# A gated-linear-attention stage with its recurrence in groups of four chunks, and its first projections by halves of the tokens

## The reference

```
def gla_mixer(h, w_in, w_gate2, b_gate, norm_w, w_out):
    proj = h @ w_in
    q, k, v, r, glr = jnp.split(proj, ...)          # glr has rank 16
    log_a = jax.nn.log_sigmoid(glr @ w_gate2 + b_gate) / GLA_TAU
    g = jnp.cumsum(lac, axis=2)                     # within a chunk
    k_dec = kc * jnp.exp(g_end[:, :, None] - g)
    def body(state, inp):                           # over the 16 chunks
        state = state * jnp.exp(ge_c)[..., None] + jnp.einsum('bshk,bshv->bhkv', kd_c, v_c)
        o = jnp.einsum('bqhk,bhkv->bqhv', q_c, state)
        return state, o
    o = rms_normalize(from_chunks(o)).reshape(b_, l_, hv) * norm_w
    return (o * jax.nn.silu(r)) @ w_out
```

## Time and profile before

| | us |
|---|---|
| median of three runs | 2855.92 (2855.51 to 2856.86) |
| profiled execution | 2854.91 |
| its span | 2853.1 |
| TensorE busy in the span | 2756.6 (97%) |
| TensorE busy in 0 to 60 us | 46.50 |
| TensorE busy in 440 to 450 us, granted clock | 5.08, 0.90 |
| TensorE busy in 450 to 460 us, granted clock | 7.48, 0.50 |

### The profile page before, as it was taken

One profiled execution on the slowest core, in us unless ns is written; L12 is line 12 of the kernel. 1 busy time (PEld: TensorE's weight loads), 2 busy tenths in 40 slices (PEclk: granted clock), 3 DMA queues, 4 the chain that ended last, 5 costly groups with the idle time before them and its releaser, 6 DMA issues. The chain is left out here.

```text
span 2853.1 us, 38388 instructions
## 1 busy us (share of the span) xinstructions
PE 2756.6 (97%) x13551; PEld 2276.0 (80%) x13551; DVE 1553.9 (54%) x1958; ACT 1047.5 (37%) x1526; POOL 1611.6 (56%) x1096
## 2 busy tenths in 40 slices
PE   8999998999999999899999999999998999999998
PEld 6888886788888888678778778778786888888887
DVE  5334335455555645667667666667634544444445
ACT  4313315432333323644444444544524322222223
POOL 3333334777677776866466565565435655565552
PEclk9999998999999999999999999999999999999999
DMA  3111110112112121212111121121430211122112
GB/s 122 38 45 37 37 44 0 52 45 66 44 51 59 44 66 44 94 47 64 41 53 57 38 63 49 45 63 49 155 111 16 59 59 37 51 59 59 37 51 96
DMA packets 200726, 160.23 MB, mean 56 GB/s; under 512 B 6231, under 2 KB 176812, under 8 KB 200621
## 3 DMA queue, kind: packets, MB, share of 16 engines
q1 hardware_dynamic: 200621, 158.83, 18.5%
HBM read 143.08 MB, written 15.73 MB: 56 GB/s over the span
## 5 line engine op out<-in xcount | busy, mean ns | idle before, releaser
L339 POOL TENSOR_TENSOR w_lo<-w_raw,w_hi 128x512 fp32r<-128x512 f32 x272 | 384.6, 1420 | 238.2 <-ACT w_hi L333 238.2
L443 PE MATMUL PA<-h_hi,w_hi 128*128 128x512 f32 x816 | 331.6, 406 | 17.7 <-PEq L929 5.9
L445 PE MATMUL PA<-h_hi,w_lo 128*128 128x512 f32 x816 | 321.0, 393 | 0.0
L444 PE MATMUL PA<-h_lo,w_hi 128*128 128x512 f32 x816 | 320.5, 393 | 0.0
L339 POOL TENSOR_TENSOR w_lo<-f_sums,w_hi 128x512 fp32r<-128x512 f32 x114 | 186.4, 1635 | 172.7 <-ACT w_hi L333 172.7
L333 ACT CAST w_hi<-w_raw 128x512 fp32r<-128x512 f32 x272 | 164.0, 617 | 228.1 <-DMA w_raw<-in_w_in 118.6
L443 PE MATMUL PB<-f_t_hi,w_hi 128*128 128x512 f32 x544 | 215.5, 396 | 9.3 <-ACT hy_tm L2523 5.0
L445 PE MATMUL PB<-f_t_hi,w_lo 128*128 128x512 f32 x544 | 212.6, 391 | 0.0
L444 PE MATMUL PB<-f_t_lo,w_hi 128*128 128x512 f32 x544 | 212.3, 390 | 0.0
L339 POOL TENSOR_TENSOR w_lo<-w_lo_raw,w_hi 128x512 fp32r<-128x512 f32 x108 | 139.8, 1300 | 115.7 <-ACT w_hi L333 115.7
L443 PEld LDWEIGHTS PA<-h_hi,w_hi 128*128 128x128 f32 x816 | 155.1, 190 | 54.5 <-issue 13.8
(11 more groups left out here) (543 smaller groups left out, 7177.7 us busy)
## 6 DMA issues: line engine op xcount, KB each, us to landing
w_raw<-in_w_in SPq DMA_DIRECT2D x64, 512.0 KB, 5.3
w_raw<-in_ffn_w_up SPq DMA_DIRECT2D x42, 512.0 KB, 5.0
w_lo_raw<-in_w_down SPq DMA_DIRECT2D x64, 256.0 KB, 2.6
w_raw<-in_w_up SPq DMA_DIRECT2D x30, 512.0 KB, 5.3
w_raw<-in_gla_w_in SPq DMA_DIRECT2D x24, 512.0 KB, 3.8
w_lo_raw<-in_ffn_w_down SPq DMA_DIRECT2D x44, 256.0 KB, 2.6
X<-in_x SPq DMA_DIRECT2D x8, 512.0 KB, 7.4
w_raw<-in_gla_w_out SPq DMA_DIRECT2D x8, 512.0 KB, 3.5
```

Source lines behind the costliest of these rows:

```text
L339: pool.tensor_tensor(lo, source, hi.bitcast(F32), ALU.subtract).then_inc(self.split, 1)
L443: pe.matmul(bank, ah[:, k, :], bh[:, k, :], start=(k == 0 and not more), stop=False, skip_group_check=more)
L444: pe.matmul(bank, ah[:, k, :], bl[:, k, :], start=False, stop=False, skip_group_check=more)
L445: mm = pe.matmul(bank, al[:, k, :], bh[:, k, :], start=False, stop=(k == 3), skip_group_check=more)
```

## The change

The steps of the recurrence become groups of four chunks. `ORDER` has `C0` to `C4` in place of `C0` to `C8`: four updates in `C0`, four reads and four updates in `C1` to `C3`, four reads in `C4`. They stand two `r` tiles apart. The states of a group have four slots, which lie in `T3`; `DD` and `MM` hold four results each; ScalarE squares two tiles and takes two roots in one operation.

In the first stage the low-rank product of the first 512 tokens is laid between the transposes of the last tiles, in two parts, into `PB`. The key product of head 0's first half comes right behind the last transposes, ahead of the second half of the low-rank product, and the first gate comes after the first two of eight parts of the second half of the keys.

```diff
-            ORDER = ("k.0 C8* YR* gate k.1 YT0* v.0 v.1 YT1* v.2 v.3 dn* q.0 q.1 KT r.0 C0 r.1 C1 r.2 C2 r.3 C3 "
-                     "r.4 C4 r.5 C5 r.6 C6 YRa r.7 C7").split()
+            ORDER = ("k.0 C4* YR* gate k.1 YT0* v.0 v.1 YT1* v.2 v.3 dn* q.0 q.1 KT r.0 C0 r.1 r.2 C1 r.3 r.4 C2 "
+                     "r.5 YRa r.6 C3 r.7").split()
+            GROUP = 4
+            GROUPS = NCH // GROUP
+            def state_bank(n):
+                return c.DD[:, n % 2 * HALF + n % GROUP // 2 * DV:n % 2 * HALF + n % GROUP // 2 * DV + DV]
+            def out_bank(m):
+                return c.MM[:, m % GROUP * DV:(m % GROUP + 1) * DV]
...
-                head.tensor(pe, lambda m: None)
+                for m in range(MT - 2):
+                    norm.turn(pe, m)
+                pe.wait_ge(norm.lo, MT // 2)
+                pe.wait_ge(s["g_lo"], 1)
+                rank(0, range(KT // 2))
+                norm.turn(pe, MT - 2)
+                rank(0, range(KT // 2, KT))
+                norm.turn(pe, MT - 1)
+                key(0, range(KT))
                 pe.wait_ge(s["rows_in"], 16 * 14)
+                pe.wait_ge(norm.lo, MT - 1)
...
                 pe.wait_ge(norm.lo, MT)
-                pe.wait_ge(s["g_lo"], 1)
-                for half in range(2):
-                    cols = slice(half * HALF, (half + 1) * HALF)
-                    for k in range(KT):
-                        mm = product(pe, c.MM[:, cols], (ghi[:, k, :], glo[:, k, :]),
-                                     (c.hhi[:, k, cols], c.hlo[:, k, cols]), k == 0, k == KT - 1)
-                mm.then_inc(s["glr_mm"], 1)
+                rank(1, range(KT)).then_inc(s["glr_mm"], 1)
+                key(1, range(2))
                 pe.wait_ge(s["glr"], 1)
                 pe.wait_ge(s["params"], 1)
+                gate(0)
+                key(1, range(2, KT)).then_inc(st.used, 1)
...
                 def update(h, n):
-                    if n >= 2:
+                    if n >= GROUP and n % GROUP < 2:
                         pe.wait_ge(s["s"], h * NCH + n - 1)
...
                 def read(h, n):
                     pe.wait_ge(s["s"], h * NCH + n + 1)
                     m = n // 2
-                    if m >= 2:
-                        pe.wait_ge(s["o_n"], h * MT + m - 1)
+                    if m >= GROUP:
+                        pe.wait_ge(s["o_n"], h * MT + m // 2 * 2 - 2)
...
-                            read(h, 2 * m - 2)
-                            read(h, 2 * m - 1)
-                        if m < MT:
-                            update(h, 2 * m)
-                            update(h, 2 * m + 1)
+                            for n in range(GROUP * (g - 1), GROUP * g):
+                                read(h, n)
+                        if g < GROUPS:
+                            for n in range(GROUP * g, GROUP * (g + 1)):
+                                update(h, n)
...
+                def squares(h, g):
+                    act.wait_ge(s["o_mm"], h * NCH + GROUP * (g + 1))
+                    for m in (2 * g, 2 * g + 1):
+                        act.activation(junk[:, m % 2, :], out_bank(m), ACT.Square, accum_out=so[:, m:m + 1]).then_inc(s["o_sq"], 1)
+                    two = slice(2 * g, 2 * g + 2)
+                    act.wait_ge(s["o_ms"], h * GROUPS + g + 1)
+                    act.activation(qo[:, two], vo[:, two], ACT.Sqrt).then_inc(s["o_sd"], 1)
...
                 def state(h, n):
-                    dve.wait_ge(s["st_mm"], h * NCH + n + 1)
-                    wait(dve, s["o_mm"], h * NCH + n - 1)
+                    dve.wait_ge(s["st_mm"], h * NCH + n // GROUP * GROUP + 3 + n % 2)
+                    wait(dve, s["o_mm"], h * NCH + n - GROUP + 1)
...
+                def outputs(h, g):
+                    two = slice(2 * g, 2 * g + 2)
+                    dve.wait_ge(s["o_sq"], h * MT + 2 * g + 2)
+                    dve.tensor_scalar(vo[:, two], so[:, two], 1.0 / DV, EPS, ALU.mult, ALU.add).then_inc(s["o_ms"], 1)
+                    dve.wait_ge(s["o_sd"], h * GROUPS + g + 1)
+                    dve.reciprocal(ro[:, two], qo[:, two])
+                    dve.drain()
+                    for m in (2 * g, 2 * g + 1):
+                        dve.tensor_scalar(Y[:, m, :], out_bank(m), ro[:, m:m + 1], None, ALU.mult).then_inc(s["o_n"], 1)
```

More of the change, by code:

```diff
@@ L979, in gla @@
             G2 = sb("gla_gate2", [P, DK])
-            S = sb("gla_state", [P, 2, DV])
+            junk = sb("gla_o_junk", [P, 2, DV])
+            S = T3.rearrange("p (n v) -> p n v", v=DV)
             DEC = sb("gla_dec", [P, NCH])
@@ L1119, in _, with rank, key @@
                 pe.wait_ge(s["ident_in"], 16)
-                head.tensor(pe, lambda m: None)
+                def rank(half, ks):
+                    cols = slice(half * HALF, (half + 1) * HALF)
+                    for k in ks:
+                        mm = product(pe, c.PB[:, cols], (ghi[:, k, :], glo[:, k, :]),
+                                     (c.hhi[:, k, cols], c.hlo[:, k, cols]), k == 0, k == KT - 1)
+                    return mm
+                def key(half, ks):
+                    cols = slice(half * HALF, (half + 1) * HALF)
+                    hi, lo = (x.rearrange("p (k n) -> p k n", k=KT) for x in st.slot(0, at(0, "k")))
+                    pe.wait_ge(st.split, st.ready(0, at(0, "k")))
+                    for k in ks:
+                        mm = product(pe, c.PA[:, cols], (hi[:, k, :], lo[:, k, :]),
+                                     (c.hhi[:, k, cols], c.hlo[:, k, cols]), k == 0, k == KT - 1)
+                    return mm
@@ new lines, in gate @@
+                def gate(h):
+                    pe.wait_ge(s["g2_in"], 16 * h + 16)
+                    wait(pe, s["s"], NCH * h)
+                    for half in range(2):
+                        cols = slice(half * HALF, (half + 1) * HALF)
+                        mm = pe.matmul(c.DD[:, cols], G2, GLR[:, cols], start=True, stop=True)
+                    mm.then_inc(s["gate_mm"], 1)
+                for m in range(MT - 2):
+                    norm.turn(pe, m)
+                pe.wait_ge(norm.lo, MT // 2)
@@ L1157, in run @@
                     name, _, part = x.partition(".")
+                    if isinstance(h, int) and x in ("k.0", "gate", "k.1"):
+                        return
                     if x == "gate":
[L1159 to L1162, removed]
-                            mm = pe.matmul(c.DD[:, cols], G2, GLR[:, cols], start=True, stop=True)
-                        mm.then_inc(s["gate_mm"], 1)
+                        gate(h)
                     elif name in ("k", "q"):
@@ L1376, in run @@
                     elif x[0] == "C":
-                        m = int(x[1:])
-                        if m < MT:
-                            state(h, 2 * m)
-                            state(h, 2 * m + 1)
-                        if m >= 2:
-                            output(h, m - 2)
-                        if m >= 1:
-                            dve.wait_ge(s["o_sq"], h * MT + m)
-                            dve.tensor_scalar(vo[:, m - 1:m], so[:, m - 1:m], 1.0 / DV, EPS, ALU.mult,
-                                              ALU.add).then_inc(s["o_ms"], 1)
-                        if m == MT:
-                            output(h, MT - 1)
+                        g = int(x[1:])
+                        if g < GROUPS:
+                            for n in range(GROUP * g, GROUP * (g + 1)):
+                                state(h, n)
+                        if g >= 1:
+                            outputs(h, g - 1)
                     elif x in ("YRa", "YR"):
```

30 lines of the change are left out of this document (9 added, 21 removed).

## The result

The changed kernel takes 2841.01 us (median of four runs, 2835.57 to 2843.93), before 2856.39 on the same chip: a ratio of 0.9943, 95% interval 0.9928 to 0.9958. The forecast was 2844.8, 11.1 us less; it became 15.4 less, half a microsecond outside the range of 2841.5 to 2851.0, on the faster side. The direction and the place of the gain were right, its size was too small.

A forecast was written before the change was run, and what follows sets the result against it. TensorE, busy 97% of the span, was taken as the bound. First stage 4.5, three passages between heads 4.9 and last head 1.7 sum to 11.1 us less, giving 2844.8; range 2841.5 to 2851.

The forecast's parts named there:

- The step of the recurrence: Recurrence, `C1` to `C3`: four reads and four updates take 2.25 us each, a pair appended costing 0.43.
- The place of the table load and Abs: Gate chain after a head's last reads: table load between last squares and root, Abs 3.64 us behind the reads, before 2.72.
- The end of the last head: Last head, silu to transposes: 6.0 us in place of 6.57; with 1.16 gained before it, together 1.7.
- A wait of 1.3 appears at `v.2`: First stage: TensorE would reach `v.2` at 64.3, `kd` allows 65.6; gains behind the gate are lost, leaving 4.5 us.
- at nothing: GpSimd and the transfers: same steps in same order, all their waits for things that come earlier too, so no effect on time.
- So `YT1` comes 0.92 later than before: Passage to a next head: chain later by 0.92 us against the reads, net gain 1.63 for each of three passages.
- I take 4.0, the middle: First stage: TensorE stays at half clock 4.0 us after dense matmuls begin, between 2.72 and 5.29 seen, costing 1.9 us.
- Each pair keeps its whole price: Rival, recurrence: appended pairs cost 0.58 or 0.64, not 0.43; 5.8 us less gain, 2850.6; chance 0.17.
- Half clock as long as now: Rival, first stage: transposes hold the clock back until 34.88, so the stage gives 1.5 us: 2847.8; chance 0.15.
- Slower: Rival: new waits at `v.2` and `YT1` drop TensorE's clock, four slow stretches cost 23 us; 12 slower, 2868; chance 0.04.
- Nothing gained: Rival: whole price of pairs and long half clock together leave 2.3 us, 2853.6; chance 0.04.
- appended reads keep their whole price: Recurrence, from the skill's weight-load rule: appended reads cost 0.58, 2.4 us less gain over four heads, or 2847.

## Why the prediction was right or wrong

**Right.** That TensorE is the bound and only borders, gaps and waits pay. The step of the recurrence, 2.25 forecast, 2.26 measured, and 2.5 us per head up to the last reads. The place of the table load and Abs 3.64 behind the reads (3.58). That TensorE has no wait for parameters, weights or states. That the change adds no slow stretch of its own. The end of the last head: 6.0 from the silu to the transposes, measured 434.99 - 429.26 = 5.73.

**Wrong, the step that failed:** "`kd` follows ScalarE's Abs, which stood at 53.35 and moves by 4.5 with the gate: 65.6. A wait of 1.3 appears at `v.2`." The chain does not move as a block. Within it stood a subtraction of 2.54 us that I took as it was, though `kd` itself, of the same size, takes 1.22 in the earlier trace rows. 1.3 of it was waiting for GpSimd, whose part I had put "at nothing" because it has the same steps in the same order. But GpSimd's split starts with the end of the key product, not with Abs. The new order has 18 matmuls between the gate and that end where 24 were, so the split comes 1.3 us earlier against the gate (6.17 behind it in place of 7.51), and has only 0.1 left to run when the subtraction starts. The chain got 1.3 shorter (`kd` ends 17.37 behind the gate in place of 18.67), exactly as much as the wait would have been. `v.2` still starts within 0.1 of `kd`'s end, by chance: TensorE needs 17.42 by its own pace.

**Wrong by the same cause:** "So `YT1` comes 0.92 later than before." Abs came 0.86 later against the reads, but the split only 0.41 (8.61 behind them in place of 8.20), since it follows TensorE's own two reads more; so the subtraction waited 0.45 less and the chain was late by only 0.41. That is 0.5 for each of three passages, 1.5 us.

**Mis-sized:** "I take 4.0, the middle" for half clock in the first stage. It was 2.7 there and between 1.4 and 3.1 in the ten profiles of this order; where in this span a run falls is luck, but 4.0 lies outside all ten. The transposes were mis-sized too: I took the 1.03 of their row for their pace, but the row ends later than the next starts, and a tile takes 0.79; the parameters took 0.2 and not 0.5. With all this the gate came 5.9 earlier and not 4.5: 1.4 us.

Together 1.3 + 1.5 + 1.4 = 4.2, and 11.1 + 4.2 = 15.3, near the 14.93 by which the last head's transposes moved; the 0.4 between them I have not traced. What comes behind them differs from one profile of the same kernel to the next, by 2.6 us in the two of the changed kernel.

**Rivals.** *Each pair keeps its whole price*: fell with the step of 2.26. *Half clock as long as now*: fell; the matmuls reach full clock at 27.3, before the next tile's transposes. In the one profile of the kernel with the product behind them, the clock even rose within the transposes, with no dense matmul ahead. The rule that I had put beside this rival, from the Trainium skill ("TensorE: Matmul & The Clock Gate", Part 4: PE-mode transpose), does not agree with that profile. *Slower*: fell. Its wait was made by holding GpSimd back, 1.58, and was followed by full clock. *Nothing gained*: fell with the first two. That appended reads keep their whole price, 0.58, and the time becomes 2847, fell too: a step of four takes 2.26 and not 2.40, and the order of the halves changes nothing. The rule of the Trainium skill on weight loads, "TensorE: Matmul & The Clock Gate" (Part 3, The mechanism), by which they would keep it, is not borne out here.

**The range.** I added bounds on the low side for the clock and the chain at `YT1`, but none for a chain that gets shorter. The length of the subtraction was treated as fixed, and the low end came out 0.5 too high.

## What to carry to other kernels

An operation whose record is twice as long as that of its like in the same trace (2.54 against 1.22 here) may hold a wait within it, and a change of order moves the two engines of that wait against each other: look up what the other engine did in that time before moving the chain as a block. Small matmuls of another shape cost their borders, about 0.5 us a step here; group them as far as banks allow. Two waits of TensorE, 5.4 and 2.5 us, which could not be removed, cost another 4.2 us in half clock behind them; matmuls whose results are thrown away brought these back.

## What the runs showed of the hardware

- An unsplit float32 matmul of 256 columns on half of the array costs 0.21 to 0.24 us each in a row: 0.24 behind one on the same rows (updates issued twice), 0.21 for each of a pair appended in turn on the two halves. The full array takes 0.86 for 512 columns (the gate), 0.43 for 256 by that. Why half an array takes half the time was not tried.
- VectorE's operation with two inputs in SBUF ended 1.08 to 1.13 us behind GpSimd's in six places, though it had started 0.1 to 2.1 us before GpSimd's end; the wait stands inside its record. GpSimd's own splits grew from 1.9 and 2.4 to 3.85 and 4.26 beside VectorE's work, and a running sum of VectorE from 2.29 to 4.33 beside GpSimd's.
- The clock rose at different times in the same order: 1.4 to 3.1 us behind the first dense matmul in ten profiles with the low-rank product between the transposes, 2.7 and 4.4 in two of the old order, and within a tile's transposes in the one with the product behind them. The granted clock of the profile read 1.00 in stretches of the first stage where the matmuls came 0.43 apart.
